# Decode attention with a running maximum inside a batch, and three output merges in place of eight

## The chip, the core and the metric

The kernel runs on one core of a Trainium2 chip. TensorE (PE) does the matmuls and the 128x128 transposes, which are matmuls with a constant matrix. VectorE (DVE) and ScalarE (ACT) read its results from PSUM. GpSimd (POOL) and SyncE (SP) issue most of the DMA transfers here. The metric is the device time of one execution in microseconds; lower is better.

## What is computed

One layer of a decoder: an input projection, gated linear attention, differential attention, an output projection, a SwiGLU network and a gated embedding, for a prompt of 1024 tokens and for 8 decode batches of 8 new tokens each. The change lies in the differential attention. A prompt head (4 heads, two sub-heads `c` each) attends causally over the prompt. A decode batch attends over 4096 cached keys, 32 pages of 128 that a page table names, and over its own new keys:

```python
def diff_attend_sample(q, k, v, lam, k_past, v_past):
    ...
    s_past = jnp.einsum('bqhcd,bkhcd->bhcqk', q, k_past).astype(F32) * scale
    s_new = jnp.einsum('bqhcd,bkhcd->bhcqk', q, k).astype(F32) * scale
    s_new = jnp.where(jnp.tril(jnp.ones((T, T), dtype=bool)), s_new, -jnp.inf)
    a = jax.nn.softmax(jnp.concatenate([s_past, s_new], axis=-1), axis=-1)
    w = (a[:, :, 0] - lam * a[:, :, 1]).astype(v.dtype)
    return (jnp.einsum('bhqk,bkhv->bqhv', w[..., :P], v_past)
            + jnp.einsum('bhqk,bkhv->bqhv', w[..., P:], v))
```

All of it is fp32. The cached keys and values that are read come to 134 MB.

## The kernel before

`attention` (from line 1347) is one block in which every engine runs its own instruction list, written out by a loop over steps `t`. Semaphores tie the lists together; nothing is reordered at run time, so an engine that waits holds up all that stands behind it in its list.

Decode is cut into 64 groups of four pages, 8 groups (`NG`) for each of the 8 batches. A group needs 1 MB of keys and 1 MB of values. Prompt attention is cut into 32 units (a head and a block of 128 queries against 1 to 8 key blocks), and one unit takes two steps. So step `t` holds, on PE: the transposes of key group `t`, four heads of four each (`turn_keys`, line 1615); a piece of the prompt's weights turned (1588) or of the prompt's output (1597); the transposes of the decode weights of group `v = t - LAG` (`turn_p`, 1650); the prompt's scores (1575); the decode scores of group `t-1` (`score`, 1627); and the output products of group `v` (`values`, 1669). `LAG` is `NG + 1 = 9`: the softmax of a batch uses one maximum over all of its 4096 + 64 scores, so no weight of a batch can be made before its last score. There are 74 steps.

PSUM has eight banks. Banks 0 and 1 hold prompt scores, 5 prompt weights, 6 the decode scores (`S_BANK`), 7 the decode output (`O_BANK`). Banks 2 to 4 are a ring that every transpose passes through (`Ring`): PE may fill a slot only when the use three places earlier has been copied out. ACT copies out the key heads 0 to 2 (`take_keys`, 1498), DVE head 3 (1779) and the weights (`take_p`, 1818). In a batch's last step there are more uses: `new_s` (scores against the new keys, 1637), `new_p` (their weights turned, 1644) and `merge` (1677).

The way of a group's scores is: PE fills `S_BANK`; DVE takes their maximum (`max_scores`, 1784) and copies them to the SBUF tile `dec_s` (`copy_scores`, 1790), which frees the bank. After a batch's last group `take_new` (1800 to 1806) adds the mask to the new keys' scores, joins all maxima and writes the bias. From then on ACT makes the weights of that batch, one group a step, from `dec_s` (`exps`, 1509; for the new keys 1514). The products of the batch's eight groups accumulate in `O_BANK`; `final_scale` (1824 to 1828) and `finalize` (1835) scale them into `dec_osc`, `merge` adds the two sub-heads' rows with a matmul, and ACT copies the 32 rows to `dec_os` (1520).

Transfers: key pages arrive in a ring of `KR = 4` groups, issued by SP (`load_pages`, 1331; group `n` when group `n-4` has been turned), value pages in `VR = 4` groups, issued by POOL when the group four earlier has been used. The first three key groups are loaded in an earlier stage. SP's list also has the prompt's queries and keys, the prompt's values (1414) and, when the last unit's product is done, the first two tiles of the output weights for the next stage (1432), which POOL scales after its last value page (1456). After the block all engines meet at a barrier and the next stage begins on ACT with line 2146.

```python
            for t in range(STEPS):
                v = t - LAG
                n, c = divmod(t, 2)
                first_group = 0 <= v < NKV and v % NG == 0
                if 0 <= v < NKV and not first_group:
                    exps(v)
```

## Time and profile before

| | |
|---|---|
| median of 3 runs | 1874.31 us (1873.79 to 1874.56) |
| the profiled execution | 1873.89 us |
| its span | 1872.2 us |
| PE busy | 1763.7 us, 94% of the span |
| DVE busy | 1190.8 us, 64% |
| ACT busy | 735.2 us, 39% |
| moved by DMA | 265.77 MB |

The profile has these views. The page gives busy time per engine and 40 slices of the span. The table by stretch gives, for any stretch, the busy time of each engine, the clock that PE was granted as a share of full speed, the busy share of the 16 DMA engines and the bytes per second. The list by shape gives the mean duration of one instruction. The list of waits says who waited for whom. The timeline gives the instructions in order of time, with the idle time of the engine ahead of one and what ended it in square brackets. "PEld" is PE's weight load, "SPq" SP's DMA queue. In a name such as `psum<-consts,dec_k` the tile written stands ahead of the arrow.

### The profile page before, as it was taken

The numbers are of one execution on the slowest core, as the hardware profiler recorded it, in microseconds if no ns is written. First come the engines' busy times: TensorE is split into PE (matmuls) and PEld (weight loads), VectorE is DVE, ScalarE is ACT, GpSimd is POOL, SyncE is SP. The second block draws the span as 40 slices with busy tenths as digits, with TensorE's granted clock in tenths as the row PEclk, the third lists the DMA queues.
The fourth block names the chain that finished last, engine by engine and source line by source line (L and its number), as shares of the span: only waits on it lengthen the run. The fifth ranks groups of instructions, "written<-read, shape, count | busy, mean of one in ns | idle before, by whom it ended". The sixth has DMA issues, their size and how long they took to land.

```text
span 1872.2 us, 35531 instructions
## 1 busy us (share of the span) xinstructions
PE 1763.7 (94%) x13086; PEld 1629.1 (87%) x13086; DVE 1190.8 (64%) x1947; ACT 735.2 (39%) x1417; POOL 343.5 (18%) x360
## 2 busy tenths in 40 slices
PE   6999999996999999986999999999999999999997
PEld 6999998984666667665998999999999999999997
DVE  4223643475777777765449866676677878799543
ACT  5113323563565656653325233222232434245320
POOL 1111331001233333332111212111211000000110
PEclk9999999898999999998999999999999999999999
DMA  5323561228999999976111222222222424232121
GB/s 164 108 81 82 142 152 46 88 57 265 325 353 354 341 362 360 346 232 218 35 45 46 81 77 74 81 70 75 76 70 70 158 79 136 74 106 86 47 71 48
DMA packets 233019, 265.77 MB, mean 142 GB/s; under 512 B 16210, under 2 KB 173524, under 8 KB 232852
## 3 DMA queue, kind: packets, MB, share of 16 engines
q1 hardware_dynamic: 212084, 195.41, 33.3%
q0 software_dynamic: 20768, 68.17, 10.6%
q8 instruction: 101, 1.65, 0.4%
q14 instruction: 66, 0.54, 0.1%
HBM read 229.84 MB, written 29.21 MB: 138 GB/s over the span
## 4 chain that ended last, share of the span: by engine, by line
PE 45%; DVE 6%; ACT 1%; issue 1%; DMA 1%; POOL 0%; DVEq 0%; ACTq 0%
PE psum L2546 33%; PE psum L151 10%; DVE x_second_lo L2560 1%; DVE unit_lo L1938 1%; DMA x_first_hi_raw<-scratch_z 1%; PE psum L2225 0%; DVE x_second_lo_raw L2564 0%; PE psum L2922 0%; DVE rstd_and_products L2604 0%; DVE x_first_lo L2560 0%; DVE h L2604 0%; ACT unit_hi L1932 0%; DVE rstd_and_products L2037 0%; DVE x_lo L2254 0%; DMA w_raw<-in_w_ple_gate 0%
## 5 line engine op out<-in xcount | busy, mean ns | idle before, releaser
L2546 PE MATMUL psum<-x_second_hi,unit_hi 128*128 128x364 f32 x924 | 304.3, 329 | 8.0 <-DVE x_second_lo L2560 4.6
L2546 PE MATMUL psum<-x_second_lo,unit_hi 128*128 128x364 f32 x924 | 303.1, 328 | 0.0
L2546 PE MATMUL psum<-x_second_hi,unit_lo 128*128 128x364 f32 x924 | 303.1, 328 | 0.0
L1331 POOL DMA_DIRECT2D dec_v<-in_cache_v x256 | 138.0, 539 | 288.0 <-issue 282.5
L151 PE MATMUL psum<-x_hi,w_hi 128*128 128x364 f32 x744 | 177.8, 347 | 7.1 <-DVE x_lo L2254 7.1
L2546 PEld LDWEIGHTS psum<-x_second_hi,unit_hi 128*128 128x128 f32 x924 | 173.7, 188 | 10.8 <-issue 5.6
L2546 PE MATMUL psum<-x_first_hi,unit_hi 128*128 128x364 f32 x528 | 173.7, 329 | 1.7 <-DVE x_first_lo L2560 1.7
L2546 PEld LDWEIGHTS psum<-x_second_hi,unit_lo 128*128 128x128 f32 x924 | 173.7, 188 | 0.0
L2546 PEld LDWEIGHTS psum<-x_second_lo,unit_hi 128*128 128x128 f32 x924 | 173.6, 188 | 0.0
L2546 PE MATMUL psum<-x_first_hi,unit_lo 128*128 128x364 f32 x528 | 173.5, 329 | 0.0
L2546 PE MATMUL psum<-x_first_lo,unit_hi 128*128 128x364 f32 x528 | 173.2, 328 | 0.0
L1932 ACT ACTIVATE unit_hi<-unit_sums 128x512 fp32r<-128x512 f32 (+1 forms) x136 | 83.3, 618 | 219.6 <-PE psum L2546 187.7
L1498 ACT ACTIVATE dec_kt<-psum 128x512 f32<-128x512 f32 x192 | 108.6, 599 | 154.9 <-PE psum L1615 154.9
L151 PE MATMUL psum<-x_hi,w_lo 128*128 128x364 f32 x744 | 164.9, 330 | 0.0
L151 PE MATMUL psum<-x_lo,w_hi 128*128 128x364 f32 x744 | 164.5, 329 | 0.0
L2425 POOL TENSOR_TENSOR w_raw<-w_raw,gains 128x1024 f32<-128x1024 f32 x42 | 89.6, 2132 | 377.4 <-DMA w_raw<-in_w_ffn_gate 209.3
L1615 PE MATMUL psum<-consts,dec_k 128*128 128x128 f32 x1024 | 139.5, 281 | 20.5 <-DMA dec_k<-in_cache_k 9.3
L1932 ACT ACTIVATE unit_hi<-w_raw 128x512 fp32r<-128x512 f32 (+1 forms) x136 | 82.5, 617 | 175.9 <-PE psum L2546 155.8
L1615 PEld LDWEIGHTS psum<-consts,dec_k 128*128 128x128 f32 x1024 | 115.3, 143 | 39.5 <-issue 14.9
L151 PEld LDWEIGHTS psum<-x_hi,w_hi 128*128 128x128 f32 x744 | 127.7, 189 | 15.3 <-DVE x_lo L2254 7.4
L151 PEld LDWEIGHTS psum<-x_lo,w_hi 128*128 128x128 f32 x744 | 129.7, 189 | 0.0
L151 PEld LDWEIGHTS psum<-x_hi,w_lo 128*128 128x128 f32 x744 | 129.6, 189 | 0.0
(319 smaller groups left out, 3320.5 us busy)
## 6 DMA issues: line engine op xcount, KB each, us to landing
dec_k<-in_cache_k SPq DMA_DIRECT2D x256, 256.0 KB, 5.4
dec_v<-in_cache_v POOLq DMA_DIRECT2D x256, 256.0 KB, 5.3
w_raw<-in_w_in SPq DMA_DIRECT2D x25, 512.0 KB, 3.9
scratch_z<-ffn_hidden SPq DMA_DIRECT2D x22, 546.0 KB, 2.8
w_raw<-in_w_ffn_gate SPq DMA_DIRECT2D x22, 512.0 KB, 3.8
w_raw<-in_w_ffn_up SPq DMA_DIRECT2D x22, 512.0 KB, 3.8
w_raw<-in_w_ffn_down SPq DMA_DIRECT2D x16, 512.0 KB, 3.9
feat_swap<-feat_n SPq DMA_DIRECT2D x32, 136.5 KB, 2.4
```

What stands on the lines that cost most here:

```text
L151: ins = pe.matmul(out[:, c, 0:SPAN], w(k), x(k)[:, c * SPAN:c * SPAN + SPAN], start=n == 0 and w is whi and x is xhi, stop=n == len(ks) - ...
L1331: eng.dma_start(ring[:, slot, p:p + 1, :], cache[bass.ds(page, 1)].rearrange("o t f -> t o f")).then_inc(sem, 16)
L1498: act.activation(m.kt[:, t % 2, h, :], ring_bank(("keys", t, h)), ACT.Copy).then_inc(d["ring_act"], 1)
L1615: ins = pe.transpose(ring_bank(key)[:, p * P:p * P + P], m.kr[:, t % KR, p, h * P:h * P + P], ident)
L1932: act.activation(m.uhi[unit][:, 0:half_tiles(t), :], unit_source(m, t, unit), ACT.Copy).then_inc(s["w_hi"], 1)
L1938: dve.tensor_tensor(m.ulo[unit][:, 0:n, :], unit_source(m, t, unit), f32(m.uhi[unit][:, 0:n, :]), ALU.subtract).then_inc(s["w_lo"], 1)
L2425: gp.tensor_tensor(m.raw[:, u], m.raw[:, u], gain(m, "ffn").unsqueeze(2).broadcast_to([P, KT, P]), ALU.mult).then_inc(s["w_scaled"], 1)
L2546: ins = pe.matmul(bank[b], w[unit][:, j, :], x[slot][:, j, :], start=start and j == 0 and w is m.uhi and x is m.xhi7, stop=j == k - 1 and ...
L2560: dve.tensor_tensor(m.xlo7[slot][:, 0:n, :], source, f32(m.xhi7[slot][:, 0:n, :]), ALU.subtract).then_inc(s["x_lo"], 1)
```

## The change

- **Running maximum.** The bias of group `g` is the smaller of the bias before and of that group's own `-SC * maximum`, written by one small DVE instruction right behind the maximum (after's line 1835). ACT makes the weights of a group straight from `S_BANK` one step after its scores (`exps(t - 2)`, 1537); `copy_scores` and the tile `dec_s` are gone. `LAG` is 3, and there are 68 steps.
- **Output so far.** Each group's product now stands alone in `O_BANK`. DVE adds it in the next step to an SBUF tile, which it first scales by `fade = exp(new bias - old bias)` (`add_output`, 1874 and 1870); ACT makes `fade` with an exponential of one column (1545). At a batch's end ACT makes eight `share` factors, with which the sums of the groups are weighted (`final_scale`, 1883 to 1891).
- **New keys.** Their scores are made in step `8b-2` (1675), before the batch's first maximum, and give its first bias; their weights are made, turned and multiplied with the batch's fourth group (`NEW = 3`).
- **Merges.** `finalize` writes into `dec_os`, and three matmuls of 4, 3 and 1 batches with their copies replace eight.
- **Waits.** PE's next scores wait for ACT's exponential (`exp_done`), not for DVE's copy (`s_taken`), and PE's `values` wait for `add_output` (`summed`).
- **Order.** On ACT `prompt_exps(t-1)` comes first in a step, ahead of the key copies; on DVE `prompt_combine` comes ahead of `take_keys`. The four `norm_prompt` of DVE stand behind the last step, where they stood in steps 68 to 71.
- **Transfers.** Both rings have 5 groups. Value group 0 is issued at once and groups 1 to 4 with key groups 1 to 4. On SP the new keys' values and the queries come ahead of key group 3. The output weights are issued as soon as the last but one unit's weights have been turned.

```diff
-    m.kr, o = m.at("dec_k", o, [P, KR, 4, H * P])
-    m.vr, o = m.at("dec_v", o, [P, VR, 4, H * P])
+    kr, o = m.at("dec_k", o, [P, 4, 4, H * P])
+    vr, o = m.at("dec_v", o, [P, 4, 4, H * P])
...
-    m.ss, o = m.at("dec_s", o, [P, PAST + NS])
+    k4, o = m.at("dec_k_more", o, [P, KR - 4, 4, H * P])
+    v4, o = m.at("dec_v_more", o, [P, VR - 4, 4, H * P])
...
-    m.os, o = m.at("dec_os", o, [32, DB, DV])
+    oo, o = m.at("dec_o_so_far", o, [P, DV])
+    m.oacc = oo[:, :]
+    m.sn, o = m.at("dec_s_new", o, [P, NS])
+    m.os, o = m.at("dec_os", o, [P, DB, DV])
...
-KR, VR, QR, PRE = 4, 4, 4, 3
+KR, VR, QR, PRE = 5, 5, 4, 3
 NG = NPG // 4
 NKV = DB * NG
-LAG = NG + 1
+LAG = 3
 STEPS = NKV + LAG + 1
...
+NEW = 3
+MERGES = ((0, 4), (4, 7), (7, 8))
...
+def merge_at(t):
+
+    b, last = divmod(t - LAG - NG, NG)
...
+        for n, (_, end) in enumerate(MERGES):
+            if end == b + 1:
+                return n
+    return None
...
+def new_at(t):
+
+    b, r = divmod(t + 2, NG)
+    return 0 if t == 0 else b if r == 0 and 0 < b < DB else None
...
+            sp.dma_start(m.vs[0:NS, :], io["new_v_sample"]).then_inc(d["new_v_in"], 16)
             sp.wait_ge(ids_in, 16)
+            for n in range(2, QR):
+                load_queries(sp, m, scr, n, q_in[n])
             for n in range(PRE, KR):
                 load_pages(sp, m.table, io["cache_k"], m.kr, n, k_page_in[n], n)
-            for n in range(2, QR):
-                load_queries(sp, m, scr, n, q_in[n])
-            sp.dma_start(m.av[:, :, :], io["new_v_prompt"].rearrange("(c p) f -> p c f", p=P)).then_inc(head_v_in, 16)
-            sp.dma_start(m.vs[0:NS, :], io["new_v_sample"]).then_inc(d["new_v_in"], 16)
+                if n == PRE:
+                    sp.dma_start(m.av[:, :, :], io["new_v_prompt"].rearrange("(c p) f -> p c f", p=P)
+                                 ).then_inc(head_v_in, 16)
...
-            sp.wait_ge(s["o_done"], NU)
+            sp.wait_ge(s["turned"], pieces_before(NU - 1))
...
-            sp.wait_ge(d["ring_act"], ring.emptied["merge", DB - 1])
+            sp.wait_ge(d["ring_act"], ring.emptied["merge", len(MERGES) - 1])
...
             for n in range(NKV):
-                if n < VR:
-                    gp.wait_ge(d["ring_filled"], ring.filled(("keys", 2 * n, H - 1)))
-                else:
+                if 0 < n < VR:
+                    gp.wait_ge(d["ring_filled"], ring.filled(("keys", n, H - 1)))
+                elif n:
                     gp.wait_ge(d["pv_done"], n - VR + 1)
                 load_pages(gp, m.table, io["cache_v"], m.vr, n % VR, v_page_in[n % VR], n)
...
-            def exps(v):
...
-                act.wait_ge(d["s_taken"], v + 1)
-                if v >= 2:
-                    act.wait_ge(d["ring_filled"], ring.filled(("p", v - 2)))
-                act.activation(m.pg[:, v % 2, :], m.ss[:, 512 * g:512 * g + 512], ACT.Exp, scale=SC,
...
+            def exps(k):
...
+                act.wait_ge(d["negm"], k + 1)
...
+                act.activation(m.pg[:, k % 2, :], S_BANK, ACT.Exp, scale=SC, bias=bias,
+                               accum_out=esum[:, u, g:g + 1]).then_inc(d["exp_done"], 1)
+                if g == NEW:
...
+                if g:
+                    act.activation(fade[:, u, g:g + 1], negm[:, u, g - 1:g], ACT.Exp, scale=-1.0, bias=bias
...
+            def shares(b):
...
+                act.activation(share[:, u, 0:NG], negm[:, u, 0:NG], ACT.Exp, scale=-1.0, bias=negm[:, u, NG - 1:NG]
...
-                first_group = 0 <= v < NKV and v % NG == 0
-                if 0 <= v < NKV and not first_group:
-                    exps(v)
+                k = t - 2
+                prompt_exps(t - 1)
                 if t < NKV:
                     take_keys(t, 0)
                     take_keys(t, 1)
                 if c == 1 and 0 <= n - 1 < NU:
                     copy_weights(n - 1, 0)
-                prompt_exps(t - 1)
-                if first_group:
-                    exps(v)
+                if 0 <= k < NKV:
+                    exps(k)
+                    if k % NG == NG - 1:
+                        shares(k // NG)
                 if c == 0 and 0 <= n - 2 < NU:
                     copy_out(n - 2)
...
-                if t >= LAG + NG and (t - LAG - NG) % NG == 0:
-                    copy_os((t - LAG - NG) // NG)
+                if merge_at(t) is not None:
+                    copy_os(merge_at(t))
...
-                if g == 0:
-                    pe.wait_ge(d["qb_ready"], 2 * b + 2)
                 if k:
-                    pe.wait_ge(d["s_taken"], k)
+                    pe.wait_ge(d["exp_done"], k)
...
-                if g == 0:
+                if v:
+                    pe.wait_ge(d["summed"], v)
+                if g == NEW:
...
-                    else:
-                        pe.wait_ge(d["final"], 4 * b)
...
-            def merge(b):
-                pe.wait_ge(d["final"], 4 * b + 4)
-                emptied(("merge", b))
...
+            def merge(n):
+
+                a, b = MERGES[n]
+                pe.wait_ge(d["final"], 5 * b)
+                emptied(("merge", n))
+                pe.matmul(ring_bank(("merge", n))[0:32, 0:(b - a) * DV], const(m, "merge"), m.os[:, a:b, :],
...
-                if t >= LAG + NG and (t - LAG - NG) % NG == 0:
-                    merge((t - LAG - NG) // NG)
+                if merge_at(t) is not None:
+                    merge(merge_at(t))
...
-                    if v % NG == 0:
+                    if v % NG == NEW:
...
-                if t and t % NG == 0 and t // NG <= DB:
-                    score_new(t // NG - 1)
+                if new_at(t) is not None:
+                    score_new(new_at(t))
...
-                dve.tensor_reduce(mx[:, g:g + 1], S_BANK, AX.X, ALU.max)
-
-            def copy_scores(k):
-                b, g = divmod(k, NG)
-                if b:
-                    dve.wait_ge(d["exp_done"], k - NG + 1)
-                dve.tensor_copy(m.ss[:, 512 * g:512 * g + 512], S_BANK).then_inc(d["s_taken"], 1)
+                dve.tensor_reduce(mx, S_BANK, AX.X, ALU.max).then_inc(d["mx_done"], 1)
...
+                before = neg_new if g == 0 else negm[:, u, g - 1:g]
...
+                dve.scalar_tensor_tensor(negm[:, u, g:g + 1], mx, -SC, before, ALU.mult, ALU.min).then_inc(d["negm"], 1)
...
+            def add_output(v):
...
+                dve.wait_ge(d["pv_done"], v + 1)
+                if g == 0:
...
+                    dve.tensor_copy(m.oacc, O_BANK[:, 0:DV]).then_inc(d["summed"], 1)
...
+                    dve.scalar_tensor_tensor(m.oacc, m.oacc, fade[:, b % 2, g:g + 1], O_BANK[:, 0:DV], ALU.mult, ALU.add
...
-                dve.tensor_reduce(ssum[:, 0:1], esum[:, b % 2, :], AX.X, ALU.add).then_inc(d["final"], 1)
...
+                dve.wait_ge(d["share_done"], b + 1)
...
+                dve.tensor_tensor(share[:, u, 0:NG], share[:, u, 0:NG], esum[:, u, 0:NG], ALU.mult
...
+                dve.tensor_reduce(ssum[:, 0:1], share[:, u, 0:NG], AX.X, ALU.add).then_inc(d["final"], 1)
...
+                dve.reciprocal(ssum[:, 1:2], ssum[:, 0:1]).then_inc(d["final"], 1)
...
-                dve.wait_ge(d["final"], b * 4 + 3)
-                dve.wait_ge(d["pv_done"], NG * b + NG)
-                if b:
-                    dve.wait_ge(d["ring_filled"], ring.filled(("merge", b - 1)))
-                dve.tensor_scalar(m.osc[:, :], O_BANK[:, 0:DV], cs[:, 1:2], None, ALU.mult).then_inc(d["final"], 1)
+
+                dve.wait_ge(d["final"], b * 5 + 4)
+                dve.wait_ge(d["summed"], NG * b + NG)
+                dve.tensor_scalar(m.os[:, b, :], m.oacc, ssum[:, 1:2], cs[:, 0:1], ALU.mult, ALU.mult).then_inc(d["final"], 1)
...
                 if t >= LAG + NG and (t - LAG - NG) % NG == 0:
+                    add_output(v - 1)
                     finalize((t - LAG - NG) // NG)
                 if 0 <= t - 2 < NKV:
                     max_scores(t - 2)
-                if 0 < t - 1 <= NKV and (t - 1) % NG == 0:
-                    take_new((t - 1) // NG - 1)
-                if 0 <= t - 2 < NKV:
-                    copy_scores(t - 2)
+                if 0 < v <= NKV and v % NG:
+                    add_output(v - 1)
+                if t and new_at(t - 1) is not None:
+                    take_new(new_at(t - 1))
+                if c == 0 and 0 <= n - 1 < NU:
+                    prompt_combine(n - 1)
                 if t < NKV:
                     take_keys(t, 3)
                 if t == 0:
                     weigh_lambda()
                 if 0 <= v < NKV:
-                    if v % NG == 0:
+                    if v % NG == NEW:
                         take_new_p(v // NG)
                     take_p(v)
-                if c == 0 and 0 <= n - 1 < NU:
-                    prompt_combine(n - 1)
                 prompt_maxima(t)
                 if t % NG == 4 and t // NG + 1 < DB:
                     queries(t // NG + 1)
                 if t >= LAG + NG - 1 and (t - LAG - NG + 1) % NG == 0:
                     final_scale((t - LAG - NG + 1) // NG)
-                if HALVES < t <= HALVES + H:
-                    norm_prompt(t - HALVES - 1)
+            for h in range(H):
+                norm_prompt(h)```

On DVE, in the step that follows a batch's last score (before: step 17, the second batch begins). `att_small` holds maxima, sums and biases, `dec_osc` the scaled output:

```order
L1824 TENSOR_REDUCE att_small<-att_small 128x1
L1826 RECIPROCAL att_small<-att_small 128x1
L1828 TENSOR_TENSOR att_small<-att_small 128x1
L1835 TENSOR_SCALAR dec_osc<-psum,att_small 128x128
L1784 TENSOR_REDUCE att_small<-psum 128x1
L1800 TENSOR_TENSOR dec_s<-psum,consts 128x64
L1802 TENSOR_REDUCE att_small<-dec_s 128x1
L1804 TENSOR_REDUCE att_small<-att_small 128x1
L1806 TENSOR_SCALAR att_small<-att_small 128x1
L1790 COPY dec_s<-psum 128x512
L1779 COPY dec_kt<-psum 128x512
```

After, the new keys of a batch are taken in a step of their own, before that batch's first maximum:

```order
L1826 TENSOR_REDUCE att_small<-psum 128x1
L1835 SCALAR_TENSOR_TENSOR dec_running<-att_small,dec_running 128x1
L1874 SCALAR_TENSOR_TENSOR dec_o_so_far<-dec_o_so_far,dec_running,psum 128x128
L1844 TENSOR_TENSOR dec_s_new<-psum,consts 128x64
L1847 TENSOR_REDUCE att_small<-dec_s_new 128x1
L1849 TENSOR_SCALAR att_small<-att_small 128x1
L1819 COPY dec_kt<-psum 128x512
```

The batch's last sums, its scaled output and the join of the maxima no longer stand in one row with the new keys, and the 128x512 copy into `dec_s` is gone; the small instruction of line 1835 and the sum of line 1874 have come in.

On PE around the same place, before:

```order
L1637 MATMUL psum<-dec_new_k,dec_qb 32x64 x4
L1669 MATMUL psum<-dec_v,dec_pt 32x128 x16
L1615 MATMUL psum<-consts,dec_k 128x128 x8
L1588 MATMUL psum<-consts,att_p 128x128 x4
L1615 MATMUL psum<-consts,dec_k 128x128 x8
L1677 MATMUL psum<-dec_osc,consts 32x128
L1644 MATMUL psum<-consts,dec_pn 128x128
L1650 MATMUL psum<-consts,dec_p 128x128 x4
```

and after:

```order
L1654 MATMUL psum<-consts,dec_k_more 128x128 x8
L1682 MATMUL psum<-consts,dec_pn 128x128
L1688 MATMUL psum<-consts,dec_p 128x128 x4
L1614 MATMUL psum<-att_k_107,att_q 128x384 x2
L1664 MATMUL psum<-dec_kt,dec_qb 32x512 x4
L1675 MATMUL psum<-dec_new_k,dec_qb 32x64 x4
L1700 MATMUL psum<-dec_new_v,dec_ptn 32x128 x4
L1707 MATMUL psum<-dec_v,dec_pt 32x128 x16
```

Before, the new keys' scores, the merge and the new keys' weights follow each other in one step's length; after, the weights that are turned belong to the batch whose scores have long been made, and the scores to the next one.

On ACT in an even step, before:

```order
L1509 ACTIVATE dec_p,att_small<-dec_s,att_small 128x512
L1498 ACTIVATE dec_kt<-psum 128x512 x2
L1474 ACTIVATE att_p,att_small<-psum,att_small 128x256
L1490 ACTIVATE att_o<-psum,att_small 128x128
L1491 ACTIVATE att_o_sq,att_o_ss<-psum,att_small 128x128
L1498 ACTIVATE dec_kt<-psum 128x512
```

and after:

```order
L1501 ACTIVATE att_p,att_small<-psum,att_small 128x2x2x128
L1525 ACTIVATE dec_kt<-psum 128x512 x2
L1537 ACTIVATE dec_p,dec_running<-psum,dec_running 128x512
L1545 ACTIVATE dec_running<-dec_running 128x1
L1517 ACTIVATE att_o<-psum,att_small 128x128
L1518 ACTIVATE att_o_sq,att_o_ss<-psum,att_small 128x128
L1525 ACTIVATE dec_kt<-psum 128x512
```

The prompt's exponential has moved ahead of the key copies, and the decode exponential behind them; it reads `psum` now.

## Rows read from the trace of the kernel before

**Rows 1.** Page, part 2: 40 slices of 46.8 us.

```profile
DMA  5323561228999999976111222222222424232121
```

**Rows 2.** Timeline of PE: the output products of decode groups 0, 7, 8, 15, 16, 32, 54.

```profile
488.92 1.06 PE L1669 MATMUL psum<-dec_v,dec_pt 128*32 128x128 f32 x32
530.26 1.06 PE L1669 MATMUL psum<-dec_v,dec_pt 128*32 128x128 f32 x32
538.40 1.06 PE L1669 MATMUL psum<-dec_v,dec_pt 128*32 128x128 f32 x32
580.42 1.06 PE L1669 MATMUL psum<-dec_v,dec_pt 128*32 128x128 f32 x32
589.06 1.06 PE L1669 MATMUL psum<-dec_v,dec_pt 128*32 128x128 f32 x32
689.21 1.06 PE L1669 MATMUL psum<-dec_v,dec_pt 128*32 128x128 f32 x32
825.09 1.06 PE L1669 MATMUL psum<-dec_v,dec_pt 128*32 128x128 f32 x32
```

**Rows 3.** Table by stretch: us, busy per engine with counts, PE clock, DMA share, GB/s.

```profile
500.00:600.15 100.15, 93.92 (x1172) 69.75 (x1170) 74.52 (x159) 60.16 (x156) 34.50 (x64) 1.00 1.02 353
...
689.00:730.00 41.00, 40.27 (x509) 30.75 (x505) 29.79 (x59) 25.03 (x63) 14.19 (x27) 1.00 1.04 368
```

**Rows 4.** Waits, 440 to 860 us: who, for whom, us, times, longest.

```profile
PE psum L1575 <- ACT att_p L1474: 11.0, 24, 1.0
...
PE psum L1615 <- DVE dec_s L1800: 6.1, 7, 1.0
PE psum L1644 <- ACT dec_kt L1498: 5.8, 6, 1.0
```

**Rows 5.** Timeline: queues and PE at the stage's head.

```profile
438.48 3.64 SPq L1331 DMA_DIRECT2D dec_k<-in_cache_k  x4
...
455.94 1.57 PEld L1615 LDWEIGHTS psum<-consts,dec_k 128*128 128x128 f32 x8 [10.22 <-DMA dec_k<-in_cache_k]
```

**Rows 6.** DMA answers: bytes from 500 to 800 us; key landings from 660 to 666.

```profile
DMA packets 47479, 105.47 MB, mean 352 GB/s; under 512 B 7033, under 2 KB 10105, under 8 KB 47421
...
dec_k<-in_cache_k SPq DMA_DIRECT2D x4, 256.0 KB, 12.0
```

**Rows 7.** List by shape, 500 to 820 us: mean ns of one.

```profile
L1498 ACT ACTIVATE dec_kt<-psum 128x512 f32<-128x512 f32 x154 | 87.0, 600 | 114.0 <-PE psum L1615 114.0
...
L1509 ACT ACTIVATE dec_p<-dec_s,att_small 128x512 f32<-128x512 f32 x52 | 38.2, 735 | 1.7 <-DVE att_small L1806 1.7
...
L1790 DVE COPY dec_s<-psum 128x512 f32<-128x512 f32 x51 | 34.7, 681 | 0.0
...
L1741 DVE TENSOR_REDUCE att_small<-psum 128x1 f32<-128x1024 f32 x12 | 14.7, 1224 | 0.4
...
L1474 ACT ACTIVATE att_p<-psum,att_small 128x1024 f32<-128x1024 f32 x12 | 13.5, 1125 | 0.0
...
L1753 DVE SCALAR_TENSOR_TENSOR att_small<-att_small 128x1 f32<-128x1 f32 x26 | 5.7, 220 | 0.9
...
L1835 DVE TENSOR_SCALAR dec_osc<-psum,att_small 128x128 f32<-128x128 f32 x6 | 2.1, 351 | 0.2
```

**Rows 8.** Timeline of the stage's end, 834 us to the next stage.

```profile
834.64 1.69 PE L1669 MATMUL psum<-dec_v,dec_pt 128*32 128x128 f32 x32 [0.32 <-DVE dec_pt L1818]
...
836.26 2.38 PE L1597 MATMUL psum<-att_v,att_wt 128*128 128x128 f32 x10
...
850.23 0.54 POOL L1331 DMA_DIRECT2D dec_v<-in_cache_v  x1 [0.61 <-issue]
...
852.11 1.22 DVE L1763 TENSOR_TENSOR att_o<-att_o,att_o_ss 128x1024 f32<-128x1024 f32 x1
...
858.12 1.08 PE L1669 MATMUL psum<-dec_v,dec_pt 128*32 128x128 f32 x32 [1.76 <-DMA dec_v<-in_cache_v]
...
863.67 1.06 ACT L2146 ACTIVATE w_hi<-w_raw 128x1024 fp32r<-128x1024 f32 x1 [3.23 <-PEq L1405]
```

109 lines of the change are left out of this document (66 added, 43 removed).

## The prediction

> **What bounds the kernel now.** I read the slices of the page first. From slice 10 on, for eight slices, DMA shows 8 or 9 tenths, and nowhere else does it [rows 1]: that is the attention stage, the only one where transfers can set the pace. PE is busy there too, so the next question is which of the two waits. The start times of the output products come next. Group v's products stand at the end of step v+9, so they are a clock of the steps. Groups 0, 16 and 32 stand at 488.92, 589.06 and 689.21: 16 steps take 100.15 us each time, 6.26 a step [rows 2]. A transfer-bound loop would hardly repeat to a hundredth; this one is paced by the engines' own lists. In that stretch PE is busy 93.9 of 100.15 us [rows 3], so its work is 5.87 us a step and its idle time 0.39. The waits say where that goes: per batch about 0.9 us for the new keys' slot, which DVE empties late (6.1 us in 7 times), 1.0 us behind the ACT copies ahead of the new keys' weights (5.8 in 6), and elsewhere 11.0 us in all for the prompt's exponential [rows 4]. No wait of that size for a page is among them in the middle of the stage. The two ends are different. At the head PE stands still for 10.2 us until key group 4 has landed at 455.94 [rows 5]. At the end, keys are finished after step 63, at 826.15 (products of group 54 at 825.09 and 1.06 long, rows 2), and nine more steps run with values alone until 859.2 [rows 8].
>
> **The sum** follows the place where the next stage's first instruction stands, 863.67 in the profiled execution [rows 8]; the work behind it is not touched, so what that point moves by, the end moves by.
>
> **Head.** Steps 0 to 3 are bound by PE and by transfers as before, and step 4 still needs key group 4. Its last issue ended at 442.12 and it landed 13.8 us later, behind the prompt's values [rows 5]. SP now issues the queries and new values first, then groups 3 and 4, and ends about 3 us sooner; POOL adds value groups 0 to 2 to the traffic where before it had two groups there. These work against each other: up to 3 us sooner, up to 1 MB at about 350 GB/s (3 us) later. I take 455. The values of groups 0 and 1 are worked inside steps 3 and 4 and hide behind this wait.
>
> **Steps 4 to 63.** These are 60 steps, and each now holds the full work, values included; before, steps 4 to 8 held none. PE's work is the same to within a few matmuls: five fewer merges out of eight. *Low end:* if every wait goes, 5.87 us. *High end:* 6.26, the mean of before. Between them: the two batch steps of a period of 16 are 8.14 and 8.64 us (530.26 to 538.40 and 580.42 to 589.06), the others (100.15 - 16.78) / 14 = 5.955 [rows 2]. The change takes the batch steps' two waits of about 0.95 each away, since the new keys are taken one step ahead of their batch and their weights come from an exponential of the step before. That gives (100.15 - 3.8) / 16 = 6.02. The prompt's exponential now comes first on ACT: at best another 11.0 / 64 = 0.17 goes.
>
> What comes in: on DVE a 128x512 copy goes (0.68 us a group) and a one-column instruction (0.22) and a 128x128 sum (near 0.35) come [rows 7], so DVE, at 74.5 of 100.15 [rows 3], has slightly less to do. The fade on ACT is one column; the nearest row is 0.22 on DVE, I take 0.2, and ACT at 60.2 of 100.15 has room. Its exponential reads PSUM instead of SBUF; I take the same 0.735, since a prompt exponential of 1024 columns out of PSUM takes 1.125, no more per column [rows 7]. The new wait is that of PE's scores for ACT's exponential of the group before. From the end of the prompt's scores the chain at its longest is: maximum 1.22, exponential 1.12, two key copies and a weight copy of the same size at 0.6 each, the decode exponential 0.74 [rows 7]; for mask, bias and the two sums between them I add 1.0, from the one-column row of 0.22. In all 5.8 to 5.9. PE's list from there to the same point of the next step is a whole step, 5.9 to 6.1. The margin is thin in the widest units and near 1 us in the narrow ones, so I charge nothing for it but do not take the 0.17 either.
>
> **The transfers** are the other limit. Moved in 300 us were 105.47 MB [rows 6]; 300 us are 47.9 steps, so a step needs 2.20 MB. At 6.02 us that is 365 GB/s. The trace shows 353 GB/s over 100 us and 368 over 41 us [rows 3], and in one stretch the landing of a key page rises to 12.0 us [rows 6], which tells of a queue that was full for a while; the ring's slack hid it. So 365 lies just inside what was seen. I add 0.03 for it: **6.05 us a step, 60 steps, 363 us**, and step 63 ends at 818.
>
> The Trainium skill bears on this: "HBM Reference", section Specifications, gives a core some 358 GB/s when both cores of a pair stream, and says that a core streaming alone measures well above it. By the first, a step would take 6.14 us and the stage 5 us more than my sum, which lies inside the second rival below; the trace's 368 over 41 us goes against a hard limit at 358 here.
>
> **End.** Four more steps stand where ten stood. Before, POOL's issue paced part of them: one page each 1.15 us (0.54 and 0.61 idle, rows 8), 4.6 us a group. After, the last value group is issued at step 61 and is there in time. Before, groups 54 and 56 lie 9.55 us apart (825.09 and 834.64), two steps without keys but with a batch's work and waits, some 2 us of it; so steps 64 and 65 take 3.7 each. Step 66 has the last prompt output, 2.4 if the clock falls as it did there, then the turning, copy and product of group 63, the last up to 1.7 [rows 8], together near 5. So group 63's products end 12 us after step 63 (10.5 to 13.5): 830. Behind them come the last sum and scale (0.35 each, rows 7), the merge, its copy and two small prompt instructions on ACT, which I estimate at 1.3 from the rows of 0.35 and 0.22, and then four `norm_prompt` of 1.22 each [rows 8], which before lay beside the value steps and now lie bare: 6.9; then the barrier and the waits between, which I take at 1.6. That is 8.5 us, where before it was 863.67 - 859.20 = 4.5. The output weights come earlier and POOL scales them in the shade. The next stage starts at **838.5**.
>
> **Merges alone.** Five fewer small matmuls and five fewer copies of under 0.4 us each (a 128x128 DVE row is 0.35, rows 7), and their places in the ring: at most 4 us were they all bare, and in steps whose waits are already counted. I give them nothing of their own.
>
> **Result.** 863.7 - 838.5 = 25.2 us less: 1873.9 - 25.2 = 1848.7 for an execution like the profiled one. The median lies 0.4 above it, so **1849**.
>
> **Rivals.**
> *All waits go.* ACT's new order removes the prompt's stalls too and the transfers keep up: 5.9 us a step is 354, 9 us less: 1840. For it: the new order on ACT has slack in the narrow units, and PE waits for nothing else. Against: 2.20 MB in 5.9 us is 373 GB/s, above each long row.
> *The transfers set the pace.* If the queues hold only 353 GB/s [rows 3], a step takes 6.23 us whatever the engines do, 374 in all, 11 more: 1860. For it: DMA share 1.02 and a landing that climbs to 12.0. What remains then is what the two ends give.
> *The change leaves the steps as they are.* Waits only change names (slots behind the new keys in step 8b-1, `summed`, `exp_done`): 6.26 a step, 375.6, 12.6 more: 1861. It can't be told from the last by the time, only by who is waited for.
> *The score bank holds PE up (slower).* One bank serves the scores, and PE may refill it only after DVE's maximum, the one-column bias and ACT's exponential, where before a DVE copy did. If this ends later than PE's list by d in each step, the gain of 25 us is gone at d = 0.42 us (25 / 60) and it is slower by over 0.2% at 0.48, that is from 6.53 us a step. At 6.6 us: 33 us over my sum, 1882. For it: the chain of 5.8 to 5.9 has only semaphore gaps to spare in the widest units. Against: half of the units are narrow, with maximum and exponential 1.2 us shorter together, and the bank's chain may run beside the next step's key transposes.
>
> **How the numbers follow.** The forecast, 1843 to 1856, gets 0.45; all waits gone 0.18; the transfers' pace 0.17; the steps as they are 0.11; something between these and before 0.03; slower 0.06. The ends of the range come from the step's bounds and those of head and end: low 5.87 a step with an end 1.5 shorter and a head 2 sooner, 1849 - 10.8 - 3.5 = 1835; I stop at 1838, since all three together are rare. High 6.26 with 2 us more at the end, 1864; I stop at 1862. What a measurement of this kernel can tell from no change is about 0.2%, 3.7 us. Faster by more than that 0.93, the same 0.02, slower 0.05.
>
> **What would show it.** The profile after should have key group 4 awaited until 453 to 458; 16 steps in 96 to 98 us; no idle of PE for the new keys' slot near 0.9 and none for their weights; DMA at 360 to 368 GB/s in the middle; the last products at 828 to 832 and four `norm_prompt` bare behind them; line 2146 at 836 to 841. Wrong would be: idle of PE's weight loads for key pages all along (the transfers), PE ahead of the decode scores idle for ACT's exponential in most steps (the bank), or the next stage held by something else than DVE's norms.

## The result and the profile after

The changed kernel takes **1865.99 us** (median of 6 runs, 1862.12 to 1867.24); the kernel before took 1874.05 in the same session (6 runs, 1871.97 to 1874.98). The ratio is 0.995, 95% interval 0.9936 to 0.9964: faster by about 8 us, where 25 were forecast. The execution profiled took 1867.0 us (span 1865.4), the one before 1873.9 (span 1872.2).

The place that the prediction follows, the next stage's first instruction on ACT, moved from 863.67 [rows 8] to 855.81, 7.9 us of the 25.2 forecast. Split at the prediction's own steps, from the rows below:

| step of the sum | forecast | measured | off |
|---|---|---|---|
| step 4 starts | 455 | 458.96 | +4.0 |
| steps 4 to 63 | 363 | 373.0 (to 831.98) | +10.0 |
| to the end of group 63's products | 12 | 16.4 (to 848.39) | +4.4 |
| to the next stage | 8.5 | 7.4 | -1.1 |

Against the kernel before, all of the 7.9 us are won behind step 63: from its end to the next stage it was 37.5 us (826.15 to 863.67) and is 23.8 now. The head lost 3.0 (455.94 to 458.96) and steps 4 to 63 lost 2.8 (370.2 to 373.0), though before, steps 4 to 8 held no output products.

The page's slices of the changed kernel, DMA share in tenths and GB/s, 46.6 us each, answer to [rows 1]:

```profile
DMA  5323561228999999973111222222222424232121
GB/s 164 108 81 83 142 153 46 87 59 274 358 372 343 368 346 369 366 247 125 45 35 57 73 79 82 70 70 81 70 70 76 152 82 134 75 107 86 48 69 48
```

The timeline of PE, output products of groups 0, 1, 29, 45 and 60, which now stand at the ends of steps 3, 4, 32, 48 and 63, and the wait at the head:

```profile
448.11 1.06 PE L1707 MATMUL psum<-dec_v,dec_pt 128*32 128x128 f32 x32
...
458.96 1.97 PE L1654 MATMUL psum<-consts,dec_k_more 128*128 128x128 f32 x8 [9.79 <-DMA dec_k_more<-in_cache_k]
...
464.94 1.06 PE L1707 MATMUL psum<-dec_v,dec_pt 128*32 128x128 f32 x32
...
641.51 1.06 PE L1707 MATMUL psum<-dec_v_more,dec_pt 128*32 128x128 f32 x32
...
737.88 1.06 PE L1707 MATMUL psum<-dec_v,dec_pt 128*32 128x128 f32 x32
...
830.92 1.06 PE L1707 MATMUL psum<-dec_v,dec_pt 128*32 128x128 f32 x32
```

Steps 33 to 48 took 96.37 us where 16 took 100.15 [rows 2]. But steps 5 to 63 took 365.98, which is 6.20 a step: the other stretches were slower. The waits from 428 to 860 us (who, for whom, us, times, longest) say why:

```profile
PEld psum L1654 <- DMA dec_k_more<-in_cache_k: 12.7, 3, 10.1
PE psum L1654 <- DMA dec_k_more<-in_cache_k: 11.9, 3, 9.8
PEld psum L1654 <- DMA dec_k<-in_cache_k: 9.1, 8, 3.4
...
PE psum L1654 <- DMA dec_k<-in_cache_k: 7.1, 5, 3.1
```

The waits of [rows 4] for the prompt's exponential have gone; in their place PE stands still for key pages. The table by stretch (us, busy of PE, PEld, DVE, ACT, POOL with counts, PE's clock, DMA share, GB/s) answers to [rows 3], and the DMA answer for 500 to 800 us to [rows 6]:

```profile
464.94:552.00 87.06, 83.54 (x1035) 63.35 (x1031) 61.67 (x150) 54.82 (x148) 33.42 (x62) 0.98 1.04 363
552.00:641.51 89.51, 84.28 (x1031) 62.30 (x1027) 65.90 (x156) 55.53 (x147) 30.20 (x56) 0.98 1.05 355
641.51:737.88 96.37, 94.62 (x1173) 69.42 (x1169) 72.92 (x174) 62.98 (x169) 34.50 (x64) 1.00 1.04 359
```

```profile
DMA packets 49054, 108.32 MB, mean 361 GB/s; under 512 B 7241, under 2 KB 10440, under 8 KB 48995
...
dec_k<-in_cache_k SPq DMA_DIRECT2D x161, 256.0 KB, 11.8
```

Key pages now take 11.8 us to land at the median, which in [rows 6] stood for one short stretch. Over the same 300 us of the kernel before, the median was 5.5:

```profile
dec_k<-in_cache_k SPq DMA_DIRECT2D x192, 256.0 KB, 5.5
```

The queues are full until about 790 us, and what they then bring is 361 GB/s on average. It is not even. Slices of 50 us, same table:

```profile
500.00:550.00 50.00, 48.84 (x611) 37.87 (x612) 37.06 (x93) 33.20 (x92) 17.98 (x34) 1.00 1.04 371
550.00:600.00 50.00, 45.89 (x552) 32.94 (x553) 35.30 (x82) 29.17 (x79) 16.52 (x31) 0.97 1.05 347
600.00:650.00 50.00, 48.88 (x624) 37.65 (x614) 37.51 (x93) 33.26 (x91) 17.79 (x33) 1.00 1.04 367
650.00:700.00 50.00, 48.70 (x586) 34.51 (x585) 37.29 (x87) 32.20 (x87) 17.41 (x33) 1.00 1.05 348
700.00:750.00 50.00, 48.75 (x608) 36.46 (x610) 37.30 (x91) 32.00 (x88) 18.70 (x35) 1.00 1.04 370
```

The two slow slices are the ones in which SP also loads the prompt keys of the next head (`att_k`, four loads from 553.6 and four from 652.3 us). No run here moves these loads, so that they are the cause is not shown.

The stage's end, timeline, answers to [rows 8]:

```profile
832.87 3.75 POOL L1483 TENSOR_TENSOR w_raw<-w_raw,small 128x1024 f32<-128x1024 f32 x2 [8.51 <-DMA w_raw<-in_w_out]
833.03 1.75 DVE L1793 SCALAR_TENSOR_TENSOR att_small<-att_small 128x1 f32<-128x1 f32 x1
...
834.81 2.48 DVE L1796 SCALAR_TENSOR_TENSOR att_p<-att_p,att_small 128x640 f32<-128x640 f32 x1
...
838.00 1.21 PE L1707 MATMUL psum<-dec_v,dec_pt 128*32 128x128 f32 x32 [3.32 <-issue]
...
847.31 1.08 PE L1707 MATMUL psum<-dec_v,dec_pt 128*32 128x128 f32 x32 [0.83 <-issue]
...
850.88 4.63 DVE L1803 TENSOR_TENSOR att_o<-att_o,att_o_ss 128x1024 f32<-128x1024 f32 x4 [1.27 <-ACT att_o_ss L1591]
...
855.81 1.06 ACT L2209 ACTIVATE w_hi<-w_raw 128x1024 fp32r<-128x1024 f32 x1 [4.97 <-PEq L1430]
```

A one-column instruction of DVE takes 1.75 us where its like took 0.220 [rows 7], and the combination behind it 2.48, both while POOL scales the output weights. Step 64 takes 7.08 us (830.92 to 838.00) where 3.7 was forecast.

Three questions follow. Do the transfers take the steps' gain back? What did the parts of the change bring to the engines? And is the end's delay POOL's doing?

### The profile page after: what moved, and what is told of

It reads as the page before. It is cut to its first block, busy times and chain, and to the rows that moved or that the text cites. A ratio compares the mean times of both kernels' runs of the same rounds, so it can differ in the third digit from the quotient of the medians.

```text
span 1865.4 us, 35748 instructions
## 1 busy us (share of the span) xinstructions
PE 1767.5 (95%) x13076; PEld 1633.3 (88%) x13076; DVE 1187.9 (64%) x2011; ACT 746.3 (40%) x1476; POOL 343.7 (18%) x360
## 2 busy tenths in 40 slices
DMA  5323561228999999973111222222222424232121
## 4 chain that ended last, share of the span: by engine, by line
PE 45%; DVE 6%; ACT 1%; issue 1%; DMA 1%; POOL 0%; DVEq 0%; ACTq 0%
PE psum L2609 33%; PE psum L151 10%; DVE x_second_lo L2623 1%; DVE unit_lo L2001 1%; DMA x_first_hi_raw<-scratch_z 1%; PE psum L2288 0%; DVE x_second_lo_raw L2627 0%; PE psum L2985 0%; DVE rstd_and_products L2667 0%; DVE x_first_lo L2623 0%; DVE h L2667 0%; ACT unit_hi L1995 0%; DVE rstd_and_products L2100 0%; DVE x_lo L2317 0%; DMA w_raw<-in_w_ple_gate 0%
## 5 line engine op out<-in xcount | busy, mean ns | idle before, releaser
L1355 POOL DMA_DIRECT2D dec_v<-in_cache_v x208 | 112.2, 539 | 204.8 <-issue 204.2
L1654 PE MATMUL psum<-consts,dec_k 128*128 128x128 f32 x832 | 115.4, 282 | 15.5 <-DMA dec_k<-in_cache_k 7.1
L2001 DVE TENSOR_TENSOR unit_lo<-unit_sums,unit_hi 128x512 fp32r<-128x512 f32 (+1 forms) x136 | 109.2, 809 | 27.4 <-ACT unit_hi L1995 27.4
L1525 ACT ACTIVATE dec_kt<-psum 128x512 f32<-128x512 f32 x192 | 108.6, 600 | 38.0 <-PE psum L1654 37.5
## 6 DMA issues: line engine op xcount, KB each, us to landing
dec_k<-in_cache_k SPq DMA_DIRECT2D x208, 256.0 KB, 11.5
dec_v<-in_cache_v POOLq DMA_DIRECT2D x208, 256.0 KB, 6.6
dec_k_more<-in_cache_k SPq DMA_DIRECT2D x48, 256.0 KB, 11.4
dec_v_more<-in_cache_v POOLq DMA_DIRECT2D x48, 256.0 KB, 6.6
```

Of the source, the lines that this page charges most:

```text
L1355: eng.dma_start(ring[slot][:, p:p + 1, :], cache[bass.ds(page, 1)].rearrange("o t f -> t o f")).then_inc(sem, 16)
L1525: act.activation(m.kt[:, t % 2, h, :], ring_bank(("keys", t, h)), ACT.Copy).then_inc(d["ring_act"], 1)
L1654: ins = pe.transpose(ring_bank(key)[:, p * P:p * P + P], m.kr[t % KR][:, p, h * P:h * P + P], ident)
L2001: dve.tensor_tensor(m.ulo[unit][:, 0:n, :], unit_source(m, t, unit), f32(m.uhi[unit][:, 0:n, :]), ALU.subtract).then_inc(s["w_lo"], 1)
```

## Experiments on the transfers

**Half of the values, after.** Here and in the next run heads 2 and 3 of the cache's values are not loaded beyond the ring's first filling, so each step moves about 0.5 MB less; the products run on what lies in the tile.

```diff
+def load_half_pages(eng, ids, cache, ring, slot, sem, n):
...
+        eng.dma_start(ring[slot][:, p:p + 1, 0:256], cache[bass.ds(page, 1)].rearrange("o t f -> t o f")[:, :, 0:256]).then_inc(sem, 16)
...
-                load_pages(gp, m.table, io["cache_v"], m.vr, n % VR, v_page_in[n % VR], n)
+                (load_pages if n < VR else load_half_pages)(gp, m.table, io["cache_v"], m.vr, n % VR, v_page_in[n % VR], n)
```

> The changed kernel, but value groups 5 to 63 load only the first half of each row (heads 0 and 1), so heads 2 and 3 of decode use old values; the same number of transfers and instructions, 1.67 MB a step instead of 2.20. Theory (the transfers take back the gain): steps 4 to 63 took 373 us in the changed kernel, 5.92 a step where no page is awaited; they fall to 355 to 358, no wait for a key page inside the loop, and the whole falls by 14 to 20 us to 1846 to 1852. Rival (the engines' own lists are longer than worked out): the steps stay at 373, the whole at 1863 to 1867.

Measured: 1852.99 us (1852.03 to 1854.95), ratio to before 0.988 (0.9856 to 0.9904), 1 us above the range expected. Products of groups 1 and 60, and the table for 500 to 800 us:

```profile
464.27 1.06 PE L1714 MATMUL psum<-dec_v,dec_pt 128*32 128x128 f32 x32
...
818.00 1.06 PE L1714 MATMUL psum<-dec_v,dec_pt 128*32 128x128 f32 x32
```

```profile
500.00:600.00 100.00, 98.73 (x1235) 73.15 (x1233) 77.43 (x188) 65.50 (x176) 35.47 (x66) 1.00 0.93 299
600.00:700.00 100.00, 98.26 (x1224) 71.79 (x1221) 76.40 (x184) 64.89 (x175) 36.01 (x67) 1.00 0.88 279
700.00:800.00 100.00, 98.03 (x1210) 71.89 (x1212) 76.18 (x180) 65.29 (x178) 36.10 (x68) 1.00 0.83 264
```

Steps 5 to 63 take 353.73 us, 6.00 a step, and PE is busy 98 of 100 us. Behind step 4, no step waits for a page any more. Steps 4 to 63 take 360.3, where 355 to 358 was expected: the engines' part had been taken some 3 us too short. So the engines' own pace is 6.00, and the transfers add 365.98 - 353.73 = 12.3 us.

**The same cut, before.**

```diff
-                load_pages(gp, m.table, io["cache_v"], m.vr, n % VR, v_page_in[n % VR], n)
+                (load_pages if n < VR else load_half_pages)(gp, m.table, io["cache_v"], m.vr, n % VR, v_page_in[n % VR], n)
```

> The kernel before with the same cut: value groups 4 to 63 load only the first half of each row, so heads 2 and 3 of decode use old values. Theory (before, the lists set the pace and the transfers had slack): 16 steps stay at 100.15 us and the whole within 3 us of 1874. Rival (transfers were a bound there as well): it falls by 10 us or more.

Measured: 1876.15 us (1872.93 to 1881.11), ratio 0.9998 (0.9982 to 1.0014). The kernel before does not wait for transfers. (In this profile steps 25 and 33 are 1.5 us longer than in the one before, at a lower granted clock, 0.83 and 0.82 of full speed; steps 34 to 49 take 100.1 us as there.) The limit is new, though the change moves no byte more.

**A head without its wait.** Of the prompt's values only the first 128 rows go ahead of key group 4:

```diff
-                    sp.dma_start(m.av[:, :, :], io["new_v_prompt"].rearrange("(c p) f -> p c f", p=P)
+                    sp.dma_start(m.av[:, 0:1, :], io["new_v_prompt"].rearrange("(c p) f -> p c f", p=P)[:, 0:1, :]
                                  ).then_inc(head_v_in, 16)
+            sp.dma_start(m.av[:, 1:, :], io["new_v_prompt"].rearrange("(c p) f -> p c f", p=P)[:, 1:, :]
+                         ).then_inc(head_v_in, 16)
...
-                if n == 0:
-                    pe.wait_ge(head_v_in, 16)
+                if n < 2:
+                    pe.wait_ge(head_v_in, 16 * (n + 1))
```

> The changed kernel, but of the prompt's values only the first block of 128 rows is loaded ahead of key group 4 and the other 1.8 MB behind it. Theory (the transfers are full from the head on, so a wait spared at the head comes back in the loop): key group 4 is there 3 to 5 us sooner, at 454 to 456 instead of 459, but steps 4 to 63 take 2 to 4 us more, and the whole moves by 0 to 2 us. Rival (the head's wait stands alone): the whole falls by 4 to 5 us to 1861.

Measured: 1864.39 us (1860.13 to 1868.05), ratio 0.9937 (0.9916 to 0.9957), not to be told from the changed kernel. Step 4 no longer waits, but the key transposes of step 5 do (timeline of PE):

```profile
466.75 1.97 PE L1656 MATMUL psum<-consts,dec_k 128*128 128x128 f32 x8 [13.47 <-DMA dec_k<-in_cache_k]
```

Group 1's products stand 12.8 us sooner than in the changed kernel (452.19 for 464.94), but group 60's only 2.9 (827.99 for 830.92). Reordering loads in a full queue moves most of the wait, it doesn't remove it.

**Rings of four,** as before the change, the new tiles left where they are:

```diff
-KR, VR, QR, PRE = 5, 5, 4, 3
+KR, VR, QR, PRE = 4, 4, 4, 3
```

> The changed kernel (1866.0 us) with rings of four groups for keys and values in place of five. Theory (steps 4 to 50 ask for more than the queues bring, about 361 GB/s; the fifth tile holds one group of each, 2 MB, of head start, 5.8 us at that rate): the steps that wait for keys come some 2 to 6 us worse in sum, 1868 to 1872 us; the batch waits stay away (steps 1 and 9 of 16 stay 3 us shorter than before). Rival (the fifth tile only delays the first wait and the rate alone sets the end): 1865 to 1867 us.

Measured: 1857.41 us (1856.22 to 1859.83), ratio 0.9898 (0.9877 to 0.9918), where both theories had 1865 or more: a miss, and 8 us faster than the changed kernel. Part of it is luck at the end. There the combination of step 64 was at its end when POOL began (timeline of DVE and POOL):

```profile
831.13 0.89 DVE L1796 SCALAR_TENSOR_TENSOR att_p<-att_p,att_small 128x640 f32<-128x640 f32 x1
...
831.91 1.89 POOL L1483 TENSOR_TENSOR w_raw<-w_raw,small 128x1024 f32<-128x1024 f32 x1 [2.35 <-DMA w_raw<-in_w_out]
```

To take this luck away, rings of four were run with POOL's scaling held back as well (the edit stands in the section on the end):

> The changed kernel with rings of four groups and with GpSimd's scaling held back until the last group's maximum. Rings of four alone gave 1857.4 us where 1868 to 1872 was expected, and its trace shows the combination of step 64 ending at 832.0, just ahead of the scaling at 831.9: no collision. Theory (the gain of that run was the missed collision, 4 to 6 us, and the fifth tile is worth nothing within 2 us): 1857 to 1861 us, as with five tiles and the scaling late (1861.3) and as with four tiles alone. Rival (rings of four are themselves some 5 us better, and the late scaling adds its own 4.5): 1852 to 1854 us.

Measured: 1859.08 us (1856.8 to 1860.58), ratio 0.9908 (0.9889 to 0.9926). With five tiles and the scaling late it was 1861.33 (0.9918, 0.9899 to 0.9937). The intervals overlap: the fifth tiles bring nothing that could be measured. In the profiles, group 60 stands at 828.77 with four tiles where it stood at 830.92 with five, and from there to group 63 it is 10.5 us where it was 16.4: of the 8 us, nearly 6 are the missed collision. The other 2 are of the size by which the changed kernel's own median moves from session to session (1866.0 and, below, 1863.0). In the pair with the late scaling, too, group 60 stands sooner with four tiles (826.43 and 829.56); why is open.

**Loads made where the queues lie idle.** The two slices of the page ahead of the stage stand at 2 tenths of DMA (87 and 59 GB/s). Key group 3 and value groups 0 and 1 go into tiles that are free by 405 us:

```diff
-KR, VR, QR, PRE = 5, 5, 4, 3
+KR, VR, QR, PRE = 5, 5, 4, 4
...
-    m.kr = [kr[:, r] for r in range(4)] + [k4[:, r] for r in range(KR - 4)]
-    m.vr = [vr[:, r] for r in range(4)] + [v4[:, r] for r in range(VR - 4)]
+    m.kr = [kr[:, 0], kr[:, 1], kr[:, 2], k4[:, 0], kr[:, 3]]
+    m.vr = [vr[:, 3], v4[:, 0], vr[:, 0], vr[:, 1], vr[:, 2]]
...
+            load_pages(sp, m.ids, io["cache_k"], m.kr, PRE - 1, pages_in[PRE - 1], PRE - 1)
+            for n in range(2):
+                load_pages(sp, m.ids, io["cache_v"], m.vr, n, sems(f"p4_first_v_in{n}"), n)
...
-            for n in range(NKV):
-                if 0 < n < VR:
-                    gp.wait_ge(d["ring_filled"], ring.filled(("keys", n, H - 1)))
+            for n in range(2, NKV):
+                if n < VR:
+                    gp.wait_ge(d["ring_filled"], ring.filled(("keys", n - 2, H - 1)))
```

> The changed kernel (1866.0 us) with 3.1 MB of the stage's transfers made ahead of it: key group 3 and value groups 0 and 1 are loaded at about 405 us, in the stage before, where the queues lie idle (390 to 427 us) and their tiles are already free; nothing else differs but the order of two tiles in each ring. Theory (from the head to about step 50 the transfers set the end): 3.1 MB less at 361 GB/s is 8.7 us; the wait for key group 4 (to 458.96) shrinks by 3 to 4 us and the waits of steps 9, 10, 25, 26 mostly go, so 1856 to 1860 us. Rival (the waits come from how long a load takes to land when both queues are busy, not from the bytes outstanding): the waits in steps 9, 10, 25 and 26 stay, and only the head's 3 us are won, 1862 to 1864 us.

Measured: 1854.52 us (1854.14 to 1855.04), ratio 0.9884 (0.9864 to 0.9904). The table for 402 to 428 us of this kernel and, below it, of the changed one; then group 60's products of this one:

```profile
402.00:428.00 26.00, 20.65 (x192) 18.53 (x192) 14.63 (x34) 9.41 (x40) 1.66 (x2) 0.84 0.54 149
```

```profile
402.00:428.00 26.00, 20.88 (x183) 18.66 (x182) 13.58 (x29) 9.43 (x40) 0.64 (x1) 0.83 0.08 21
```

```profile
820.61 1.06 PE L1713 MATMUL psum<-dec_v,dec_pt 128*32 128x128 f32 x32
```

Group 60 stands 10.3 us earlier than in the changed kernel, and 9.0 to 9.8 earlier than in two other profiles with the changed kernel's loads (829.56 and 830.40); 3.1 MB at 361 GB/s are 8.7. So bytes taken out of the full stretch come back as time, nearly one for one. But the time is better than the range expected, and where it is won was wrong. Step 4 takes 6.8 us in place of 16.8, while steps 5 to 63 take 367.06, no less than before, and step 25 alone 10.67. The waits inside the loop did not go.

## Experiments on the parts

**Eight merges,** the rest as changed:

```diff
-MERGES = ((0, 4), (4, 7), (7, 8))
+MERGES = tuple((b, b + 1) for b in range(DB))
```

> The changed kernel (1866.0 us) with one merge for each batch again, eight in all, each 128 columns wide, everything else as changed: what the second part of the change is worth alone. In the changed kernel steps 35 and 59, which hold the merges of four and of three batches, are 1.5 and 1.2 us longer than their like; the end has the third. Theory (merges are nearly worth nothing): the steps 11, 19, 27, 35, 43, 51 and 59 each become 0.4 to 0.6 us longer than their like, 2.8 to 4.2 us in place of 2.7, and part of that goes into waits for transfers that are there anyway, so 1865 to 1868 us. Rival (three merges in place of eight bring a good part of the 8 us gained): 1869 us or more.

Measured: 1865.67 us (1864.42 to 1866.71), ratio 0.9946 (0.9925 to 0.9966), the same as with three. But each of the steps 11, 19, 27, 35, 43, 51 and 59 is 1.5 to 1.65 us longer than its like, three times what was expected. Timeline of PE in step 19, and the wait's row for 490 to 826 us:

```profile
556.54 0.41 PE L1717 MATMUL psum<-dec_os,consts 128*32 128x128 f32 x2
...
558.05 0.63 PE L1688 MATMUL psum<-consts,dec_p 128*128 128x128 f32 x4 [1.11 <-ACT dec_os L1558]
```

```profile
PE psum L1688 <- ACT dec_os L1558: 7.7, 7, 1.1
```

A merge's work is small (0.41); what costs is that PE waits 1.1 us for its copy before the next bank of the ring is free, and this is the same for a merge of one batch or of four: steps 35 and 59 of the changed kernel carry 1.5 and 1.65 too. Five of these gone are 8.0 us of engine time. They do not show in the whole, since with slower engines less is waited for pages: what the steps that wait for pages have over their like is 5.1 us in all there and 12.3 in the changed kernel, and steps 5 to 63 take 366.8 us with eight merges and 365.98 with three.

**ACT's order undone:** the prompt's exponential behind the key copies again.

```diff
-                prompt_exps(t - 1)
                 if t < NKV:
                     take_keys(t, 0)
                     take_keys(t, 1)
                 if c == 1 and 0 <= n - 1 < NU:
                     copy_weights(n - 1, 0)
+                prompt_exps(t - 1)
```

> The changed kernel (1866.0 us) with one part of its new order on ScalarE undone: the prompt's exponential stands behind the key copies and the first weight copy again, as before the change, and everything else stays. Theory (that order is what took 0.43 us from steps 7, 11 and 15 of each 16, 1.3 us in 16 steps, and the waits for the prompt's exponential): those steps go back to 6.07, 5.81 and 5.92 us, TensorE waits for att_p again by some 5 to 11 us in all, and since transfers take most of what the engines gain, the time moves by 0 to 4 us: 1866 to 1870. Rival (the running maximum alone removed that wait): steps 7, 11 and 15 stay at 5.64, 5.38 and 5.48.

Measured: 1881.07 us (median of 9, 1879.93 to 1884.04), ratio 1.0026 (1.0017 to 1.0036): slower than the kernel before, and far outside what was expected. Groups 13 and 29's products, ends of steps 16 and 32, and DVE's wait from 500 to 800 us:

```profile
543.89 1.08 PE L1707 MATMUL psum<-dec_v,dec_pt 128*32 128x128 f32 x32 [0.62 <-issue]
...
645.75 1.08 PE L1707 MATMUL psum<-dec_v_more,dec_pt 128*32 128x128 f32 x32 [0.62 <-issue]
```

```profile
DVE att_small L1791 <- ACT att_p L1501: 43.0, 24, 1.9
```

Sixteen steps take 101.86 us. The change also moved DVE's `prompt_combine` ahead of its key copy (`take_keys(t, 3)`), and that one needs the exponential; when this comes late, DVE waits, then the key copy, then PE. The next run tests this reading.

**Both orders undone:** in addition `prompt_combine` stands behind `take_p` again.

```diff
-                if c == 0 and 0 <= n - 1 < NU:
-                    prompt_combine(n - 1)
                 if t < NKV:
                     take_keys(t, 3)
...
                     take_p(v)
+                if c == 0 and 0 <= n - 1 < NU:
+                    prompt_combine(n - 1)
```

> The changed kernel with both new orders undone: on ScalarE the prompt's exponential stands behind the key copies, and on VectorE the prompt's combination stands behind take_p, as before the change; running maximum, LAG of 3, rings of five and three merges stay. Undoing ScalarE's order alone gave 1881.4 us, with VectorE waiting 43 us for the prompt's exponential (500 to 800 us) in front of its key copy. Theory (the loss there is that pair: a combination ahead of the key copy needs the exponential early; with both back the loop is before's list less its batch waits, 6.02 a step): 16 steps in 96 to 98 us where 101.9 were and 94.8 are in the changed kernel, VectorE's wait for att_p gone, 1866 to 1870 us. Rival (the running maximum itself, with the score bank held until the exponential, makes the loop long whatever VectorE's order): 16 steps over 100 us, 1876 us or more.

Measured: 1866.99 us (1865.08 to 1871.28), ratio 0.9945 (0.9928 to 0.9962). Steps 17 to 32, again between groups 13 and 29:

```profile
545.81 1.06 PE L1707 MATMUL psum<-dec_v,dec_pt 128*32 128x128 f32 x32
...
643.22 1.06 PE L1707 MATMUL psum<-dec_v_more,dec_pt 128*32 128x128 f32 x32
```

That is 97.41 us, inside the 96 to 98 expected. In the run with half of the values, with both orders new, the same 16 steps take 94.79. So the pair of orders is worth 2.6 us in 16 steps, and DVE's half without ACT's is 4.5 us worse than neither. ACT's half alone was not run. In the whole the pair hardly shows, again because transfers take what the engines win: 1866.99 here, 1865.99 and 1863.03 for the changed kernel.

The whole of a period of 16 steps without transfers in the way, then: 100.15 before, 94.79 after. The orders hold 2.6. The other 2.7 can be followed step by step between the kernel before and this last run. Steps 17 and 25, in which a batch begins, take 5.37 and 5.62 us where they took 8.14 and 8.64: 5.8 less. But steps 22 and 30, which now hold the new keys, take 8.14 and 8.16 where they took 7.05 and 6.39: 2.9 more. Two merges are in what went; by their price in the changed kernel they are 3.2. By this addition, which is an estimate, the running maximum with the new keys inside the batch leaves the engines' period about where it was. It gains at the end, where four steps stand in place of ten.

## Experiments on the end, and a version that beats both

**POOL's scaling held back** until the last group's maximum has been taken:

```diff
             gp.wait_ge(gain_set, 2)
+            gp.wait_ge(d["negm"], NKV)
             for u in range(2):
                 gp.wait_ge(w_out_in[u], 16)
```

> The changed kernel, but POOL scales the output weights only after DVE has written the last decode bias. Theory (POOL's two multiplications of 1.9 us lock DVE's two-input SBUF instructions out in step 64, where a one-column one took 1.75 instead of 0.22 and the weights' combine 2.48 instead of 0.88): step 64 falls from 7.1 to about 3.7 us, PE's clock does not fall in step 65, and the whole falls by 3 to 5 us to 1861 to 1863. Rival (the stretch is DVE's own, for instance the wait for ACT): step 64 stays at 7 and the whole at 1866.

Measured: 1861.33 us (1857.74 to 1861.74), ratio 0.9918 (0.9899 to 0.9937), 4.7 us below the changed kernel's first session. The combination and the first scaling, timeline:

```profile
831.92 0.89 DVE L1797 SCALAR_TENSOR_TENSOR att_p<-att_p,att_small 128x640 f32<-128x640 f32 x1
...
834.70 1.89 POOL L1484 TENSOR_TENSOR w_raw<-w_raw,small 128x1024 f32<-128x1024 f32 x1 [11.69 <-DVE dec_running L1836]
```

DVE's combination is back at 0.89, step 64 takes 3.95 us, and groups 60 and 63 stand 10.6 us apart, not 16.4. The other profiles bear this out: in the four without the collision these groups are 10.5 to 10.6 us apart, and in the six with it (the changed order, POOL's scaling beside DVE's instructions of step 64) 13.2 to 16.4. That is the firmer evidence, since it does not depend on the session.

**The changed kernel again:**

> The changed kernel itself once more, as the standard beside the other runs of this call: 1866 us, with groups 60 and 63's products again about 16 us apart if VectorE's weight combination of step 64 falls under GpSimd's scaling, near 10.6 us if it does not.

Measured: 1863.03 us (1861.82 to 1866.42), ratio 0.9932 (0.9913 to 0.9951). Step 64 took 6.85 us, the collision, but step 65 only 2.94 where the first profile had 3.93, so groups 60 and 63 lay 13.4 us apart: neither of the two values expected. Between sessions the changed kernel's own median moves by 3 us, so differences of that size across sessions are not read here.

**All together:** the early loads, the late scaling, and the norms of heads 0 to 2 inside the loop, each once its head's eight units are done.

```diff
-                if t == HALVES:
-                    act.wait_ge(s["o_squared"], NU)
...
+                if t > 3 and t % 16 == 3:
+                    h = t // 16 - 1
+                    ss = m.a_ss[:, 0:TT - 1, h:h + 1]
+                    act.wait_ge(s["o_squared"], 8 * (h + 1))
...
+                if t > 4 and t % 16 == 4:
+                    norm_prompt(t // 16 - 1)
-            for h in range(H):
-                norm_prompt(h)
+            norm_prompt(H - 1)
```

> All that the runs so far point to, together: the changed kernel with the 3.1 MB of loads made ahead (as in the run beside it), GpSimd's scaling of the output weights held until the last group's maximum is taken (4.5 us won alone), and the prompt output's norm of heads 0 to 2 made inside the loop as each head's rows are complete, head 3's alone at the end (three of the four products of 1.16 us each that stand behind the last group, 3.5 us). Theory: 8 + 4.5 + 3.5 = 16 us below the changed kernel, 1848 to 1852 us. Rival (with the end sped up the clock falls there, or the three norms in the loop hold VectorE's queue and come back as steps): 1854 us or more.

Measured: **1848.33 us** (1847.46 to 1850.82), ratio 0.9853 (0.9835 to 0.9871), 1.5% below before and inside what was expected. The end, timeline:

```profile
834.58 1.23 DVE L1810 TENSOR_TENSOR att_o<-att_o,att_o_ss 128x1024 f32<-128x1024 f32 x1 [1.24 <-ACT att_o_ss L1596]
...
836.11 1.06 ACT L2217 ACTIVATE w_hi<-w_raw 128x1024 fp32r<-128x1024 f32 x1 [1.56 <-PEq L1434]
```

One norm stands bare where four stood, and the next stage starts 19.7 us before that of the changed kernel. It is this kernel that comes to the 1849 us once forecast for the other.

## Why the prediction was right in sign and wrong in size

**What bounds the kernel: right for before, wrong for after.** The prediction said the loop before was paced by the engines' lists; the cut of the values, which did not make it faster, shows it.

**The transfers: this is the term that failed.** "365 lies just inside what was seen. I add 0.03 for it." That is 1.8 us for 60 steps; measured are 12.3 over 59, 0.21 a step. The need was worked out rightly: 2.20 MB a step at 6.00 us ask for 367 GB/s. What was mis-sized is the supply. The 368 of [rows 3] is the mean of the 41 us from 689 to 730, most of them in a stretch that is fast in later runs too: 366 to 369 GB/s from 700 to 800 us in those with full queues. But from 550 to 600 and from 650 to 700 us the same runs have 341 to 350, and the mean of all 300 us is 360 to 362. A good stretch's rate was taken for the whole stage's. The 353 over 100 us beside it was no measure of the supply either: the loop before asked for no more (2.20 MB in 6.26 us are 351), and it did not wait. The DMA share, 1.02 then and 1.04 now, does not tell the two cases apart; the median landing does, 5.5 us then and 11.8 now. The landing of 12.0 us in [rows 6] was read as slack being used, and it was the first sign of the limit.

The rival that the transfers set the pace is what happened. That its 374 us for the 60 steps lie beside the 373.0 measured is luck: its 353 was the old loop's demand, and at 361 the same sum gives 366. Its 1860 was still too low by the head and the tail.

"HBM Reference" of the Trainium skill, section Specifications, gives about 358 GB/s a core with both cores of a pair streaming, and well above that for a core alone. Here the program ran on one core and had 361 over 300 us with full queues: the trace is near the figure for a shared pair and does not show a rate well above it for a core alone. By that figure the prediction had 6.14 a step; measured are 6.20.

**The engines' pace: right in size, wrong in its parts.** 6.02 was forecast, 6.00 measured with the transfers out of the way. But it was to come from 3.8 us in 16 steps, put down to the batch waits. Of the batch steps 5.8 did go, merges included, and 2.9 came back in the steps that hold the new keys now, for which the prediction charged nothing; the other 2.6 are the order on ACT and DVE, which it put at 0.17 a step at best and didn't count. The merges got "nothing of their own". "At most 4 us were they all bare" looked only at their own work, not at the ring's bank that waits for the copy behind each: five of them are 8.0 us of engine time. That the sum came out right is luck, from errors of opposite sign.

**The slower rival: wrong place, real danger.** It put its price on the score bank. In the changed kernel PE does not wait there. But undoing one of the two orders was enough to make the new loop slower than the old one, 101.86 us in 16 steps, by the queue of DVE.

**Head: wrong by 4.0.** Key group 4 lands at 458.96. The prediction weighed two effects, up to 3 us sooner and up to 1 MB more traffic, and had both wrong in size. Its last issue ended at 441.73, 0.4 us sooner than the 442.12 of before, not 3 (timeline of SP):

```profile
438.10 3.63 SPq L1355 DMA_DIRECT2D dec_k_more<-in_cache_k  x4
```

And POOL issued 16 value pages ahead of the landing where before it issued 8: 2.1 MB more, not 1.

**Tail: wrong by 4.4.** "POOL scales them in the shade" is the step that failed. It named the cover and didn't ask what POOL's work does to the DVE instructions beside it. In the changed kernel's second profile the miss is 1.4 us and not 4.4, so its size is not fixed. Without the collision the tail is 10.6 us, under the 12 forecast. Behind it the four norms lay bare as forecast, 4.63 us in one group; the end took 7.4 for 8.5.

**Range.** With all terms as measured, 838.5 + 4.0 + 10.0 + 4.4 - 1.1 = 855.8, and the median would have been forecast at 1866. The range ended at 1862 because its high end had 6.26 a step and 2 us at the end, and nothing for the head. These misses are not independent: in a stage with full queues the head's traffic and the loop's are one account.

## What to carry to other kernels

Before an edit that speeds a loop up, divide its bytes by the new time and compare with the mean of a long time in which the queues were full, not with the best stretch; watch how long a page takes to land and not how busy the queues are. When need and supply come near each other, look for a stage beside it in which the queues rest, and load there. Small steps in a rotating set of buffers cost the wait for their release, not their work. Orders on two engines that feed each other are to be changed and tried as a pair; here one half alone cost more than the pair won.

## What the runs showed of the hardware

**Two engines, one port.** While POOL scales `w_raw` (two SBUF inputs, 1.9 us a piece), a one-column DVE instruction with SBUF inputs took 1.75 us, not 0.22, and one of 640 columns 2.48, not 0.89; the first ended at 834.78, about when the first of POOL's two pieces was through, the second at 837.29, 0.67 us after the last of them (836.62). In the run with rings of four, DVE instructions that read PSUM ran beside the same scaling at their usual 0.68 and 0.69. "GPSIMD Engine Reference" of the Trainium skill, section Specifications, names contention with DVE instructions that have two SBUF inputs. The trace agrees, and shows in addition that a single column is enough.

**Supply of two full queues.** With 256 KB pages from two queues and the program on one core: 361 GB/s over 300 us with five tiles, 360 and 362 with four. In ten profiles with full queues the slices of 50 us from 500, 600 and 700 us have 365 to 371, those from 550 and 650 only 341 to 350; the slow ones are those with the loads of the next head's prompt keys, the cause is open. Key pages land in 11.8 us at the median then, and in 3.9 when each step moves a quarter less.

**The clock after a short stall.** PE's products of a group took 1.06 us in the loop; group 61's, at 838.00, took 1.21 and group 62's 1.94. The table by stretch of the changed kernel, PE's granted clock the third number from the end:

```profile
834.00:838.00 4.00, 0.68 (x9) 0.04 (x2) 3.96 (x4) 0.25 (x2) 2.61 (x2) 1.00 0.00 0
838.00:842.00 4.00, 3.48 (x45) 2.65 (x49) 1.69 (x4) 1.71 (x6) 0.00 (x0) 0.60 0.01 4
842.00:844.00 2.00, 2.00 (x33) 1.62 (x34) 0.07 (x1) 0.09 (x1) 0.00 (x0) 0.50 0.00 0
```

PE worked 0.68 of 4 us while DVE was held up, and was then granted 0.50, that is 1.2 GHz of 2.4. The stall does not always bring the lower clock. In the changed kernel's second profile PE worked 1.06 of the 4 us from 833 to 837, and its clock stayed full behind them:

```profile
838.00:842.00 4.00, 3.50 (x61) 2.71 (x53) 1.39 (x3) 1.80 (x6) 0.00 (x0) 1.00 0.02 4
```

Step 65 took 2.94 us there and not 3.93, and 2.93 in two further runs with the collision. So the collision itself costs some 3 us, in step 64; of the 16.4 us between groups 60 and 63 up to 3 more go with the lower clock.
